# Expert weights loaded in runs of 16 KiB per partition, with the token order that this asks for

## What is computed

```python
logits = xt @ w_router + b_router                   # (256, 32)
top_val, top_idx = lax.top_k(logits, 4)
gates = scatter(softmax(top_val))                   # (256, 32)
for e in range(32):
    hgu = xt @ w_gate_up[e] + b_gate_up[e]          # (256, 1024) @ (1024, 2048)
    gate = minimum(hgu[:, :1024], 7); up = clip(hgu[:, 1024:], -7, 7)
    y = ((up + 1) * (gate * sigmoid(1.702 * gate))) @ w_down[e] + b_down[e]
    acc += gates[:, e, None] * y                    # w_down[e]: (1024, 1024)
```

## Time and profile before

| | us |
|---|---|
| median of 3 runs | 1230.91 |
| range | 1230.85 to 1231.36 |
| the profiled execution | 1230.13 |
| its span, first to last instruction | 1228.1 |
| PE busy in it | 1110.8 (90%) |
| DVE, ACT, POOL busy | 204.9, 154.9, 18.5 |
| read from memory | 435.74 MB |

### The profile page before, as it was taken

One profiled execution on the slowest core, in us unless ns is written; L12 is line 12 of the kernel. 1 busy time (PEld: TensorE's weight loads), 2 busy tenths in 40 slices (PEclk: granted clock), 3 DMA queues, 4 the chain that ended last, 5 costly groups with the idle time before them and its releaser, 6 DMA issues.

```text
span 1228.1 us, 15468 instructions
## 1 busy us (share of the span) xinstructions
PE 1110.8 (90%) x6044; PEld 436.0 (36%) x6044; DVE 204.9 (17%) x420; ACT 154.9 (13%) x318; POOL 18.5 (2%) x68
## 2 busy tenths in 40 slices
PE   7999999868999999999999999999998999899985
PEld 6675444423333333323323333333323332233221
DVE  1301223231211111111111111111111111111111
ACT  2253230220000000000000000000000000000002
POOL 1010000000000000000000000000000000000000
PEclk9999999869999999999999999999999999999998
DMA  9923334319999999999999999999999999999994
GB/s 332 385 85 137 137 121 152 137 46 403 417 418 418 418 418 417 417 418 418 418 418 418 418 418 417 417 417 418 418 418 417 418 417 418 417 418 417 417 417 192
DMA packets 86628, 437.11 MB, mean 356 GB/s; under 512 B 7704, under 2 KB 7760, under 8 KB 53744
## 3 DMA queue, kind: packets, MB, share of 16 engines
q1 hardware_dynamic: 84880, 434.19, 87.1%
q10 hardware_dynamic: 1424, 1.57, 0.5%
q0 software_dynamic: 304, 1.06, 0.2%
HBM read 435.74 MB, written 1.06 MB: 356 GB/s over the span
## 4 chain that ended last, share of the span: by engine, by line
SPq 55%; PE 34%; issue 4%; DMA 4%; DVE 2%; ACT 1%; DVEq 0%
SPq L322 30%; SPq L317 24%; PE bank L1059 8%; PE bank L886 7%; PE bank L883 5%; PE bank L1089 3%; PE bank L983 2%; PE bank L996 2%; DMA ring<-in_w_down_dram 2%; DMA ring<-in_w_gate_up_dram 1%; PE bank L1042 1%; PE bank L1033 1%; PE bank L863 1%; PE bank L1120 1%; SPq L338 0%
## 5 line engine op out<-in xcount | busy, mean ns | idle before, releaser
L1059 PE MATMUL bank<-ring,gates 128*64 128x512 f32 x2048 | 476.1, 603 | 18.4 <-DMA ring<-in_w_gate_up_dram 15.4
L1089 PE MATMUL bank<-ring,gates 128*64 128x512 f32 x1024 | 244.2, 603 | 59.7 <-DMA ring<-in_w_down_dram 59.7
L1059 PEld LDWEIGHTS bank<-ring,gates 128*64 128x64 f32 x2048 | 134.6, 137 | 276.8 <-issue 190.7
L795 DVE TENSOR_SCALAR gates<-bank 128x512 f32<-128x512 f32 x32 | 22.1, 692 | 792.5 <-PE bank L1059 792.5
L1089 PEld LDWEIGHTS bank<-ring,gates 128*64 128x64 f32 x1024 | 63.9, 136 | 238.4 <-DMA ring<-in_w_down_dram 152.5
L886 PE MATMUL bank<-ring,colsT 128*128 128x512 f32 x192 | 84.0, 594 | 0.0
L1042 PE MATMUL bank<-gates,scatter_w 64*128 64x512 f32 x256 | 63.6, 615 | 0.8 <-ACT gates L593 0.7
L589 ACT ACTIVATE gates<-gates 128x512 f32<-128x512 f32 x32 | 20.1, 630 | 300.8 <-DVE gates L795 300.8
L1033 PEld LDWEIGHTS bank<-onehot,qkT 128*128 128x128 bf16 x1536 | 47.7, 99 | 27.9 <-issue 25.2
L883 PE MATMUL bank<-colsT,ring 128*128 128x256 f32 x256 | 56.5, 381 | 0.0
L1033 PE MATMUL bank<-onehot,qkT 128*128 128x64 bf16 x1536 | 51.5, 195 | 2.3 <-ACT qkT L574 2.3
(11 more groups left out here) (167 smaller groups left out, 458.7 us busy)
## 6 DMA issues: line engine op xcount, KB each, us to landing
ring<-in_w_gate_up_dram SPq DMA_DIRECT2D x256, 1024.0 KB, 20.8
ring<-in_w_down_dram SPq DMA_DIRECT2D x128, 1024.0 KB, 24.7
ring<-in_w_in_dram SPq DMA_DIRECT2D x10, 2048.0 KB, 19.6
ring<-in_w_out_dram SPq DMA_DIRECT2D x1, 4096.0 KB, 13.9
ring<-in_w_proj_sb_dram SPq DMA_DIRECT2D x1, 2048.0 KB, 7.3
ring<-in_w_proj_moba_dram SPq DMA_DIRECT2D x1, 2048.0 KB, 7.8
resid<-in_x_dram SPq DMA_DIRECT2D x2, 512.0 KB, 3.7
bias<-u_scratch POOLq DMA_DIRECT2D x1, 1024.0 KB, 12.5
```

The lines of the kernel that those rows point to most:

```text
L795: V.tensor_scalar(gate_t, bank[4][:, :], SWIGLU_LIMIT, None, ALU.min).then_inc(gate_rd, 1)
L1059: ins = mm(bank[4 + i][SLOTS * c:SLOTS * (c + 1), :], xeT[:, k, :], ring[:, k, i * D + c * CH:i * D + (c + 1) * CH], start=False, stop=k = ...
L1089: ins = mm(bank[6][SLOTS * c:SLOTS * (c + 1), :], rows, ring[:, KD + s, j * D + c * CH:j * D + (c + 1) * CH], start=k == 0, stop=k == KD - 1)
```

## The change

The ring has 6 slots of 16 KiB per partition (`RING = 6`, `GU = 4` of them for `gate_up`) over the same memory, and each slot is loaded by one DMA of 2 MiB in which every partition has one run of 16 KiB. A `gate_up` slot s holds rows 256s+2p and 256s+2p+1 on partition p; a `down` slot holds rows 512s+4p to 512s+4p+3. Slots are waited for and released as a whole. The contraction index is thereby permuted, so the gather reads each second column of a 256-wide block as weights, `hidden_columns` transposes each fourth column of `h_t`, and the gains come from a new small tile `gslot`, loaded by a DMA of its own in runs of two floats on ACT's queue ahead of `gfin`.

```diff
-    RING = 12
-    SLOT = 2 * D
+    RING = 6
+    GU = 4
+    SLOT = 4 * D
...
+        gslot = sb("gslot", [P, KD // 2, 2])
...
-            gu = w_gate_up[0].rearrange("e (k p) n -> e k p n", p=P)
-            dn = w_down[0].rearrange("e (k c p) n -> e k p c n", p=P, c=2)
+            gu = w_gate_up[0].rearrange("e (s p r) n -> e s p (r n)", p=P, r=2)
+            dn = w_down[0].rearrange("e (s p r) n -> e s p (r n)", p=P, r=4)
...
+                src = gu if s < GU else dn
+                q = s if s < GU else s - GU
+                piece = src[e, q] if isinstance(e, int) else src[bass.ds(e, 1), q].rearrange("o p n -> p (o n)")
+                sp.dma_start(ring[:, s, :], piece).then_inc(slot_in[s], 16)
...
-            def load_gate_up(e, done, first=0):
-                for k in range(first, KD):
-                    sp.wait_ge(gu_used, (e + done) * KD + (k + 1 - KD))
-                    load_slot(e, k)
+            def load_gate_up(e, done):
+                for s in range(GU):
+                    sp.wait_ge(gu_used, (e + done) * GU + (s + 1 - GU))
+                    load_slot(e, s)
...
             def load_down(e, done):
-                for q in range(RING - KD):
-                    sp.wait_ge(dn_used, (e + done) * (RING - KD) + (q + 1 - RING + KD))
-                    load_slot(e, KD + q)
+                for q in range(RING - GU):
+                    sp.wait_ge(dn_used, (e + done) * (RING - GU) + (q + 1 - RING + GU))
+                    load_slot(e, GU + q)
...
+                act.dma_start(gslot[:, :, :], norm_ffn_g[0].rearrange("(s p r) -> p s r", p=P, r=2)
+                              ).then_inc(late_in, 16)
...
-                                       gcol[:, KD:2 * KD].rearrange("p (k o) -> p k o", o=1)
+                                       gslot[:, :, :].rearrange("p s (r o) -> p (s r) o", o=1)
...
-                            ins = mm(bank[7][:, k * SLOTS:(k + 1) * SLOTS], pieces[i][:, t, k * P:(k + 1) * P],
+                            ins = mm(bank[7][:, k * SLOTS:(k + 1) * SLOTS], pieces[i][:, t, 2 * P * (k // 2) + k % 2:2 * P * (k // 2 + 1):2],
...
                 for k in ks:
-                    pe.wait_ge(slot_in[k], g * 16 + 16)
+                    if k % 2 == 0:
+                        pe.wait_ge(slot_in[k // 2], g * 16 + 16)
                     for i in range(2):
                         for c in range(2):
+                            n0 = (k % 2) * 2 * D + i * D + c * CH
                             ins = mm(bank[4 + i][SLOTS * c:SLOTS * (c + 1), :], xeT[:, k, :],
-                                     ring[:, k, i * D + c * CH:i * D + (c + 1) * CH], start=False,
-                                     stop=k == KD - 1)
-                    ins.then_inc(gu_used, 1)
+                                     ring[:, k // 2, n0:n0 + CH], start=False, stop=k == KD - 1)
+                    if k % 2 == 1:
+                        ins.then_inc(gu_used, 1)
...
-                    ins = tp(bank[7][:, c * P:(c + 1) * P], h_t[:, c * P:(c + 1) * P], ident[:, :])
+                    ins = tp(bank[7][:, c * P:(c + 1) * P], h_t[:, c::4], ident[:, :])
...
-                for s in range(RING - KD):
-                    pe.wait_ge(slot_in[KD + s], g * 16 + 16)
-                    for j in range(2):
-                        k = 2 * s + j
-                        rows = hT[:, k % 4, SLOTS * (k // 4):SLOTS * (k // 4) + SLOTS]
+                for s in range(RING - GU):
+                    pe.wait_ge(slot_in[GU + s], g * 16 + 16)
+                    for j in range(4):
+                        k = 4 * s + j
+                        rows = hT[:, j, SLOTS * s:SLOTS * s + SLOTS]
```

More of the change, by code:

```diff
@@ L182, in chunk_w @@
             u = PLACE[c]
-            return ring[:, 2 * u:2 * u + 2, :].rearrange("p a b -> p (a b)").rearrange("p (k n) -> p k n", k=KD)
+            return ring[:, u, :].rearrange("p (k n) -> p k n", k=KD)
         def flat(u0, u1):
-            return ring[:, 2 * u0:2 * u1, :].rearrange("p a b -> p (a b)")
+            return ring[:, u0:u1, :].rearrange("p a b -> p (a b)")
         wp_sb = flat(4, 5).rearrange("p (k n) -> p k n", k=4)
@@ L308, in _ @@
             sp.dma_start(wo_sb, w_out[0].rearrange("(k p) n -> p k n", p=P)).then_inc(wout_in, 16)
-            gu = w_gate_up[0].rearrange("e (k p) n -> e k p n", p=P)
-            dn = w_down[0].rearrange("e (k c p) n -> e k p c n", p=P, c=2)
+            gu = w_gate_up[0].rearrange("e (s p r) n -> e s p (r n)", p=P, r=2)
+            dn = w_down[0].rearrange("e (s p r) n -> e s p (r n)", p=P, r=4)
             def load_slot(e, s):
[L315 to L326, removed]
+                src = gu if s < GU else dn
+                q = s if s < GU else s - GU
+                piece = src[e, q] if isinstance(e, int) else src[bass.ds(e, 1), q].rearrange("o p n -> p (o n)")
+                sp.dma_start(ring[:, s, :], piece).then_inc(slot_in[s], 16)
+            for s in (2, 3):
+                if s == 2:
                     sp.wait_ge(unit_ps, LAST_UNIT[9] + 1)
@@ L329, in _ @@
             sp.wait_ge(out_ps, 8)
-            for s in (8, 9, 10, 11):
+            for s in (4, 5):
                 load_slot(0, s)
             sp.wait_ge(out_ps, 12)
-            for s in (0, 1, 2, 3):
+            for s in (0, 1):
                 load_slot(0, s)
-            def load_gate_up(e, done, first=0):
-                for k in range(first, KD):
-                    sp.wait_ge(gu_used, (e + done) * KD + (k + 1 - KD))
-                    load_slot(e, k)
+            def load_gate_up(e, done):
+                for s in range(GU):
+                    sp.wait_ge(gu_used, (e + done) * GU + (s + 1 - GU))
+                    load_slot(e, s)
             def load_down(e, done):
-                for q in range(RING - KD):
-                    sp.wait_ge(dn_used, (e + done) * (RING - KD) + (q + 1 - RING + KD))
-                    load_slot(e, KD + q)
+                for q in range(RING - GU):
+                    sp.wait_ge(dn_used, (e + done) * (RING - GU) + (q + 1 - RING + GU))
+                    load_slot(e, GU + q)
             def experts(done):
@@ L472, in _ @@
             act.dma_start(b_rout[:, :], b_router[0].rearrange("(e o) -> e o", o=1)).then_inc(late_in, 16)
+            with nc.allow_non_contiguous_dma(reason="two gains in a run"):
+                act.dma_start(gslot[:, :, :], norm_ffn_g[0].rearrange("(s p r) -> p s r", p=P, r=2)
+                              ).then_inc(late_in, 16)
             act.dma_start(gfin[:, :], norm_final_g.rearrange("(o d) -> o d", o=1).to_broadcast([P, D])
@@ L562, in _ @@
             act.wait_ge(logit_ps, 1)
-            act.wait_ge(late_in, 16 * 7)
+            act.wait_ge(late_in, 16 * 8)
             nc.scalar.activation(logitT, bank[0][0:E, 0:T], ACT.Identity, bias=b_rout[:, 0:1]).then_inc(logit_rd, 1)
@@ L591, in expert_rows @@
             def expert_rows(g):
-                act.wait_ge(dn_used, g * (RING - KD) + (RING - KD))
+                act.wait_ge(dn_used, g * (RING - GU) + (RING - GU))
                 nc.scalar.activation(y_t, bank[6][:, :], ACT.Copy).then_inc(y_rd, 1)
@@ L660, in _ @@
             V.memset(u_sb[:, 0:P - 1], MASKED).then_inc(u_rd, 1)
-            dve.wait_ge(late_in, 16 * 6)
+            dve.wait_ge(late_in, 16 * 7)
             whole, rest = gates[0:3 * E, 0, :], gates[0:3 * E, 1, :]
@@ L793, in hidden @@
             def hidden(e, done, prev):
-                dve.wait_ge(gu_used, (e + done) * KD + KD)
+                dve.wait_ge(gu_used, (e + done) * GU + GU)
                 V.tensor_scalar(gate_t, bank[4][:, :], SWIGLU_LIMIT, None, ALU.min).then_inc(gate_rd, 1)
@@ L1000, in _ @@
             transposes(4)
-            pe.wait_ge(late_in, 16 * 7)
+            pe.wait_ge(late_in, 16 * 8)
             pe.wait_ge(hres_rd, 4)
@@ L1082, in down @@
                 pe.wait_ge(hT_rd, g + 1)
-                for s in range(RING - KD):
-                    pe.wait_ge(slot_in[KD + s], g * 16 + 16)
-                    for j in range(2):
-                        k = 2 * s + j
-                        rows = hT[:, k % 4, SLOTS * (k // 4):SLOTS * (k // 4) + SLOTS]
+                for s in range(RING - GU):
[3 more added lines that the diff above has]
+                        rows = hT[:, j, SLOTS * s:SLOTS * s + SLOTS]
                         for c in range(2):
                             ins = mm(bank[6][SLOTS * c:SLOTS * (c + 1), :], rows,
-                                     ring[:, KD + s, j * D + c * CH:j * D + (c + 1) * CH], start=k == 0,
+                                     ring[:, GU + s, j * D + c * CH:j * D + (c + 1) * CH], start=k == 0,
                                      stop=k == KD - 1)
```

## The result

The changed kernel takes 1215.3 us in the median (1213.81 to 1216.97, four runs) beside 1231.12 us: a ratio of 0.9875 with a 95% interval from 0.9863 to 0.9886, 15.8 us or 1.3% faster. The forecast was 1211.4 us, with a range from 1205 to 1226. In a later set the changed kernel had 1215.57 us beside 1230.47, a ratio of 0.9883 [0.9861, 0.9904].

A forecast was written before the change was run, and what follows sets the result against it. The expert phase was taken as bound by the 12 MiB each expert loads. Stream -23.6, start +1.9, end +2.2 gave -19.5 us from the 1228.1 us span: 1208.6, profiled run 1210.6, median 1211.4 us; range 1205 to 1226.

The forecast's parts named there:

- The line of run lengths: Expert weight loads: 9.5 ns a packet plus 2.408 us a MiB, so 29.35 us an expert in place of 30.11.
- Rival 1: Weight stream: the line ends at 8 KiB, only down gains, 0.30 us an expert, 1225.6 us; chance 0.15.
- the halved packet price: Weight stream: a packet costs 4.7 ns, not 9.5, so the stream's gain halves to 11.8 us; 1223.2 us.
- (b): Start of the expert phase: the first slot's release, and so the first reload, comes 1.9 us later.
- (c): Stream gap at 292 to 296 us, before gate_up of expert 1: again 1.5 us, so price 0.
- (d): Slot releases from there on: about four 2 MiB pieces queued, so a release 2 us later starves nothing; price 0.
- (f): End of the kernel: last piece feeds 16 matmuls, not 8, 1.7 us more, plus PE 0.5 us late; together 2.2 us.
- `gslot`: One more DMA on ACT's queue, 8-byte runs, ahead of gfin: costliest issue there 1.50 us, so 0 to 0.5 us.
- The strided reads: Gather weight loads taken at 0, up to 4.2 us for the range; h_t transposes at most 0.6 us, range only.
- Rival 2: Gather: the strided weight load loses its cover; at 129 ns a pair 42 us slower, 1273 us; chance 0.10.

The follow-up runs named there:

- the two other mixes: Changed kernel with twelve 1 MiB slots, 8 KiB runs, gslot loaded late: 1222.62 us; changed kernel with gate_up in 4 MiB slots, 32 KiB runs: 1217.78 us.
- the late `gslot`: Changed kernel with the gslot load issued later, beside that of b_down: 1215.69 us; in a later set 1213.97 us beside the changed kernel's 1215.57.

## Why the prediction was right, and where it was off

The direction, the range and the cause were right. The time was 3.9 us over the forecast, and the profiled span 6.1 us over (-13.4, not -19.5); the median came out nearer because the profiled execution was a slow one, 1.1 us above the median where the forecast put it 0.8 us below. The forecast's own range, up to 1217, held the time partly by luck: its upper end was made of a slow gather, doubled transposes and 0.5 us for `gslot`, and what filled it was a pause, a clock and a larger `gslot`. By its steps:

- *The line of run lengths* held. 9.5 ns a packet, read from two sizes and tested on a third, gave 29.35 us an expert; 29.38 was measured, and 29.81 and 29.20 for the two other mixes became 29.81 and 29.22. Over 31 experts the forecast was 0.9 us too good. Rival 1 falls with 429 GB/s, and with it the halved packet price, the one that the Trainium skill's page "DMA: Bandwidth & Descriptors", section "Why small descriptors are slow (HBM only)", leads to: by the estimate of 4.7 ns the changed kernel would have stayed near 29.7 us an expert. The measurement decides, for a price of 9.5 ns.
- *(b) and (c), the start*: 1.9 us and no more was forecast for the grain, 1.6 measured. The size was right, the place not quite: the sum charged the first reload and put the gap at nothing, while what the rest of the stream hangs on is the issue behind the gap.
- *(d), the releases*: right within the loop, where the queue's depth covers them, wrong at its end. The step said "from there on" and was checked against a sequence in which `gate_up` comes between two loads of `down`; for the last two experts it does not. That was worth 2.8 us, and no term of the sum had it. The row that would have told it stands before the change: with four slots of 1 MiB the first of them was free at 1194.8, while the stream came to the end of expert 30 only at 1199 (PE's start at 1200.67 less the 1.7 us that lie between the last bytes and PE), 4 us to spare. With two slots of 2 MiB it is free at 1179.9, just after the stream has come to its end at 1179.5 (1181.22 less 1.7), and by the prediction's own reading of the start 1.9 us pass from a release to the bytes.
- *(f), the end*: 2.2 us were forecast and 3.4 measured. The 1.7 us for eight matmuls more were right. PE's lateness of 0.5 us did not come about, as the slot was later; in its place came the clock, 1.7 us, which the forecast had not looked at. It is not certain to fall: of the four profiles with this end, two of the changed kernel and two with the late `gslot`, three have it (waits of 2.56, 2.29 and 3.27 us) and one has not (2.75 us).
- *`gslot`*: 0 to 0.5 us was forecast; between the two profiles it is 1.6. All ten profiles give a range: from PE's first matmul of L884 to its first of L887 it takes 29.5 us in the three with the early `gslot` and 27.6 to 28.8 us in the seven without (for the kernel before L883 and L886), so 0.7 to 1.9 us. The step that failed took the dearest issue in the rows, 1.50 us, as a bound. That was behind 128-byte runs; behind 512 runs of 8 bytes the next issue took 3.98 us.
- *The strided reads*: forecast at nothing for the gather and at a little for `h_t`. The gather is at 1.51 us, its loads at 98 ns as before; the transposes take 0.68 us and not 0.59, their weight loads 209 ns and not 141. Rival 2 falls. The rule of the page "SBUF — State Buffer" of the Trainium skill, section "Door 1: The DMA port swizzle" (two hits in a line of 16 bytes are free), agrees for four hits and for one; for two hits, in the run with 32 KiB, the load took 118 ns in place of 98 and a pair 35.8 ns in place of 31.4, which is not quite free.

The groups by line of the changed kernel and of the one with 32 KiB runs, 300 to 1180 us, as in the earlier trace rows:

```profile
L1034 PEld LDWEIGHTS bank<-onehot,qkT 128*128 128x128 bf16 x1440 | 43.7, 98 | 24.3 <-issue 24.3
L1081 PEld LDWEIGHTS bank<-ident,gates 128*128 128x128 f32 x124 | 17.3, 209 | 25.1 <-issue 25.1
```

```profile
L1035 PEld LDWEIGHTS bank<-onehot,qkT 128*128 128x128 bf16 x1440 | 50.5, 118 | 24.3 <-issue 24.3
```

## What to carry to other kernels

Where a stream of loads is the bound, compare the landing intervals of pieces with different run lengths: two sizes give the price of a packet, a third tests it, and the gain of longer runs can be forecast to a few hundredths of a microsecond a piece. Larger slots then cost at the places where the order of the stream is not that of the loop: look at the last round and ask, for each slot that is reloaded, what was loaded just before it. A small DMA of tiny runs is not small for the queue that issues the next one, so put it where nothing waits behind it.

## What the runs showed of the hardware that was not expected

- The cost of the streamed loads was, for each MiB, the packets of one of the 16 queues times 9.5 ns plus 2.408 us, over runs of 2, 4, 8, 16 and 32 KiB; DMAs of 2 MiB in place of 1 MiB changed nothing (30.13 against 30.11 us an expert).
- An issue on ACT's queue behind 512 runs of 8 bytes took 3.98 us, against 0.48 us without them.
- Waits of PE of 2.29, 2.56 and 3.27 us before its last 16 matmuls were followed by the lower clock (5.35 us for the 16), and one of 2.75 us was not (3.65 us), in two profiles each of the changed kernel and of the one with the late `gslot`. At the start of the expert phase the full clock came to stay between 267 and 273 us; in four of ten profiles it had already been there before, from 260 to 263 us on, and was lost again. Two profiles of one kernel differ by 4.5 us of span, most of it by this clock.
